# The low-weight pass of a feed-forward matmul: one instruction of 512 tokens, or two of 256

## The reference, cut to what matters

```python
h = modulate(rms_norm(x, g_pre_mlp[l]), sh2, sc2)
y = jnp.square(jax.nn.relu(h @ w_ff1[l])) @ w_ff2[l]
x = x + gt2[:, None, :] * rms_norm(y, g_post_mlp[l])
```

## Time and profile before

| | us |
|---|---|
| median of 3 runs | 2076.68 |
| lowest and highest | 2076.37, 2077.79 |
| span of the profiled execution, first to last instruction | 2076.6 |
| TensorE busy | 2045.0 (98%) |
| VectorE busy | 1599.3 (77%) |
| ScalarE busy | 811.7 (39%) |

### The profile page before, as it was taken

The page is one execution under the profiler, slowest core; times in us unless marked ns, Lnnn a source line. Parts: engine busy times, 40 slices in busy tenths (PEclk is TensorE's granted clock), DMA queues, the critical chain, the costliest instruction groups (busy, mean ns, idle before and its releaser), DMA issues.

```text
span 2076.6 us, 25311 instructions
## 1 busy us (share of the span) xinstructions
PE 2045.0 (98%) x9099; PEld 1670.2 (80%) x9099; DVE 1599.3 (77%) x1843; ACT 811.7 (39%) x1063; POOL 87.7 (4%) x97
## 2 busy tenths in 40 slices
PE   7999999999999999999999999999999999999998
PEld 5787788888778778888888888888888888888886
DVE  7999897776978787687686786776867867867767
ACT  6434622224543364334243343343342433433433
POOL 1001120000220001000000000000000000000000
PEclk9999999999999999999999999999999999999999
DMA  9986568856347843233332332332333323323335
GB/s 368 391 272 194 194 205 290 298 182 201 128 171 266 274 156 112 92 106 103 106 100 91 112 102 91 119 105 97 101 100 112 101 91 111 101 91 113 107 99 197
DMA packets 181600, 324.58 MB, mean 156 GB/s; under 512 B 12601, under 2 KB 49641, under 8 KB 179233
## 3 DMA queue, kind: packets, MB, share of 16 engines
q1 hardware_dynamic: 173600, 302.08, 44.0%
q0 software_dynamic: 3568, 16.95, 2.2%
q10 hardware_dynamic: 4368, 4.73, 0.7%
HBM read 313.20 MB, written 10.52 MB: 156 GB/s over the span
## 4 chain that ended last, share of the span: by engine, by line
PE 90%; DVE 7%; ACT 1%; issue 1%; DMA 0%; DVEq 0%; ACTq 0%
PE pair L939 11%; PE pair L940 11%; PE pair L941 11%; PE pair L964 9%; PE pair L965 9%; PE pair L966 9%; PE bank L568 5%; PE bank L570 5%; PE bank L569 5%; PE bank L580 3%; PE bank L582 3%; PE bank L581 3%; DVE acc L1581 1%; DVE w_lo L1549 1%; DVE stat L1766 1%
## 5 line engine op out<-in xcount | busy, mean ns | idle before, releaser
L2017 DVE TENSOR_TENSOR yg<-yg,pair 128x1024 f32<-128x1024 f32 x240 | 289.6, 1217 | 283.2 <-PE pair L966 283.2
L939 PE MATMUL pair<-h_hi,w_lo 128*128 128x512 f32 x1020 | 397.3, 390 | 0.0
L940 PE MATMUL pair<-h_lo,w_hi 128*128 128x512 f32 x1020 | 396.8, 389 | 0.0
L941 PE MATMUL pair<-h_hi,w_hi 128*128 128x512 f32 x1020 | 396.8, 389 | 0.0
L964 PE MATMUL pair<-w_hi,op_lo 128*128 128x512 f32 x840 | 328.3, 391 | 0.0
L965 PE MATMUL pair<-w_lo,op_hi 128*128 128x512 f32 x840 | 326.9, 389 | 0.0
L966 PE MATMUL pair<-w_hi,op_hi 128*128 128x512 f32 x840 | 326.9, 389 | 0.0
L1072 ACT ACTIVATE w_hi<-raw 128x1024 fp32r<-128x1024 f32 (+1 forms) x114 | 118.3, 1045 | 270.1 <-DMA raw<-in_w_in_dram 155.2
L939 PEld LDWEIGHTS pair<-h_hi,w_lo 128*128 128x128 f32 x1020 | 191.6, 188 | 39.9 <-issue 0.2
L941 PEld LDWEIGHTS pair<-h_hi,w_hi 128*128 128x128 f32 x1020 | 191.5, 188 | 39.9
L940 PEld LDWEIGHTS pair<-h_lo,w_hi 128*128 128x128 f32 x1020 | 191.5, 188 | 39.4
(11 more groups left out here) (295 smaller groups left out, 2803.0 us busy)
## 6 DMA issues: line engine op xcount, KB each, us to landing
raw<-in_w_ada_dram SPq DMA_DIRECT2D x128, 512.0 KB, 4.6
w_raw<-in_w_ff_dram SPq DMA_DIRECT2D x128, 512.0 KB, 3.8
raw<-in_w_ff_dram SPq DMA_DIRECT2D x128, 512.0 KB, 4.4
raw<-in_w_in_dram SPq DMA_DIRECT2D x74, 512.0 KB, 4.7
gst<-in_w_ada_dram SPq DMA_DIRECT2D x64, 512.0 KB, 7.8
raw<-in_w_out_dram SPq DMA_DIRECT2D x32, 512.0 KB, 4.8
x_tok<-in_x_dram SPq DMA_DIRECT2D x4, 1024.0 KB, 8.2
xr<-in_x_dram POOLq DMA_DIRECT2D x4, 1024.0 KB, 7.0
```

The lines of the kernel that those rows point to most:

```text
L939: pe.matmul(b, lo[:, cols], h_hi[:, kt, :], start=(kt == 0), stop=False)
L940: pe.matmul(b, hi[:, cols], h_lo[:, kt, :], start=False, stop=False)
L941: last = pe.matmul(b, hi[:, cols], h_hi[:, kt, :], start=False, stop=(kt == KT - 1))
L2017: dve.tensor_tensor(y, y, pairs[2 + (i + r) % 2][:, :, :], ALU.subtract if i == 6 else ALU.add).then_inc(product_read, 1)
```

## The change

In each block of a piece the high-by-low matmul comes first and opens the accumulation for all 512 tokens. The matmul with the low part of the weights comes second, and is issued as two matmuls of 256 tokens each, with the same stationary operand, into the two halves of the same bank. The high-by-high matmul stays last. Waits and semaphores are the same. `first_piece` and the second product are not touched.

```diff
                     b, cols = pairs[m // 2][:, m % 2, :], slice(m * P, (m + 1) * P)
-                    pe.matmul(b, lo[:, cols], h_hi[:, kt, :], start=(kt == 0), stop=False)
-                    pe.matmul(b, hi[:, cols], h_lo[:, kt, :], start=False, stop=False)
+                    pe.matmul(b, hi[:, cols], h_lo[:, kt, :], start=(kt == 0), stop=False)
+                    for tok in (slice(0, 2 * P), slice(2 * P, 4 * P)):
+                        pe.matmul(b[:, tok], lo[:, cols], h_hi[:, kt, tok], start=False, stop=False)
                     last = pe.matmul(b, hi[:, cols], h_hi[:, kt, :], start=False, stop=(kt == KT - 1))
```

## The result

| | before | after |
|---|---|---|
| median, lowest and highest of 3 runs, us | 2076.68 (2076.37 to 2077.79) | 2090.79 (2090.17 to 2091.58) |
| span of the profiled execution, us | 2076.6 | 2089.0 |

The change makes the kernel 14.1 us slower, ratio 1.0068 with a 95% interval of 1.0048 to 1.0087. Run once more in a later comparison of more runs it gave 2090.74 against 2076.61, ratio 1.0071 (1.0057 to 1.0084). The span grew by 12.4 us only, because the work ahead of the feed-forward block, which is the same in both, took 1.9 us less in the profiled execution of after: its first matmul of the block starts at 748.0, and at 749.9 before. (In every run with both numbers on record, the time lies 1.8 us above its own span, so the profiled execution of before was longer than its median run by some 1.7 us.) From there to the end 14.3 us were added, near the 14.1 of the medians.

A forecast was written before the change was run, and what follows sets the result against it. TensorE's queue was taken to bound the kernel: 1020 splits at 13.3 ns add 13.5 us, 0.7 comes back from the late operand, +12.8 us gives 2089.5 us. The 8-in-10 range was 2076 to 2104 us.

The forecast's parts named there:

- The bound: In the loop TensorE is full, busy 98% of the span, so its queue's cost is nearly one to one the kernel's.
- The price of the added instruction: At line 939's 1020 split matmuls, 13.3 ns per added instruction, +13.5 us in all; chance 0.48.
- the lost beat: Rival: unequal lengths keep the stream disturbed, 5.5 ns more on each of a block's four matmuls; +36 us, 2113 us; chance 0.16.
- the per-column rival: Rival: the 13.2 ns belong to the columns, halves take 113.3 ns, the change adds 0 us, 2076.7 us; chance 0.27.
- What comes back: At line 964 the first product's late low operand is hidden by 0.053 of 0.15 us, 13 to 15 times: -0.7 to -0.8 us.
- The sum: On TensorE's queue 1020 x 13.3 ns, +13.5 us; less 0.7 come back, +12.8 us, 2089.5 us, 0.6% slower.
- Its signs of being wrong: In the trace: halves not 0.12 us apart, 512-column matmuls changing their distance, or a TensorE wait not there before.
- The order of the passes: The opening matmul reads `w_hi` and `h_lo` instead, with all four waits still ahead of it; costs nothing by itself.
- the second load: Each half at line 939 has its own weight load, 109 to 111 ns, which isn't the bound.
- the other engines: ScalarE and VectorE wait for TensorE with 26% and more idle; an iteration 0.85 us longer gives them more.
- the gain: Rival: a half costs no more than its load, a pair 218 to 223 ns; -3.6 to -8.7 us; chance 0.04.
- the slower form: Rival: 256 float32r columns run like float32, a half 213 ns, a pair 426; +204 us, 2280 us; chance 0.03.

## Why the prediction was right, point by point

**The bound.** Right for the loop. TensorE's queue sets the time there: 15.9 us of added work in it give 15.9 us once the one wait is out of the way. The first chunk is not bound by it alone; the prediction counted its 64 splits in full, and they added 0.15 us in place of 0.9.

**The price of the added instruction.** The step that the prediction called the one on which everything hangs, once per instruction or per column, came out as chosen: 13.3 ns per instruction. The rows had not decided it, as the prediction says itself; it was a choice at 0.48 against 0.27, with 0.16 for the lost beat. And the trace of after alone would have misled. Its halves are 115 ns apart, nearer to the 113.3 of the per-column rival than to 119.9, and the sign that the prediction named for it (0.120 between the halves) did not appear. Only the kernel with all passes in halves (120.0) and the one with other lengths (173 and 147) show it.

**The lost beat.** The prediction had it as a rival with 22 ns a block on top of the pair's 13.3. It does happen: the whole matmuls are 233 apart, as the earlier trace rows show behind a late load. What failed is the size. The prediction added 5.5 ns to all four matmuls; the whole ones did get 6.4 each, but in the same state the halves are 4.8 below their settled 120, and 3.3 ns a block are left: 3.4 us in all. This is the term that the forecast lacked.

**What comes back.** Forecast 0.7 us, measured 1.9: the wait cost 2.4 us before and 0.5 after. Two errors. The operand is that of the iteration's second product (it starts at 1214.68, the first at 1209.20), not of the first. VectorE's work up to it hangs on product 12, and two pieces stand between that and the second product, not one. So the operand's cover grew by 8 x 16.65 = 133 ns, and the lateness fell from 0.26 to 0.13. VectorE took as long as before, 9.88 us from the first line to the second:

```profile
1207.07 1.22 DVE L2018 TENSOR_TENSOR yg<-yg,pair 128x1024 f32<-128x1024 f32 x1 [3.67 <-PE pair L967]
...
1216.95 0.69 DVE L1985 TENSOR_TENSOR op_lo<-s_tmp,op_hi 128x512 fp32r<-128x512 f32 x1
```

The other kernels agree: with one block split (2 x 33 ns of cover) the load is 0.20 us late, and with all passes in halves (2 x 180 ns) it is on time. The second error is in the price. A load that was 0.26 us late cost 0.17 us an iteration, one 0.20 late 0.11, and one 0.13 late 0.03. So the cost falls as the lateness does, but it starts from some 0.12 us late and not from 0. That fits an estimate from rows: a load needs some 0.11 us of the matmul's 0.227, so 0.12 us are to spare.

**The sum.** 13.5 - 0.7 = 12.8 was forecast. The account is 15.9 - 1.9 = 14.0 in the loop and 0.15 in the first chunk, and 14.1 was measured. The forecast lacked 3.3 ns a block, gave back 1.2 us too little, and counted some 0.8 us in the first chunk that did not come. These errors partly cancel, so part of the closeness is luck.

**Its signs of being wrong.** It named three: halves not 0.12 apart, another distance of the 512-column matmuls, a wait that was not there. All three are in the trace of after: 0.115, 0.233, and 0.58 us once at line 939. The first two are one thing, the stream out of step, and leave the price per instruction standing; the third was not foreseen and costs little. The time came out near the forecast with the trace not looking as forecast.

**What was costed at nothing.** The order of the passes (2076.43 alone), the second load, which lies beside the matmul, and the other engines: all right. The per-column rival, the gain and the slower form are out: 256 columns run at the columns' full rate, and the load's floor of 112 ns is under 120.

## What to carry to other kernels

Where TensorE's queue is full, count instructions as well as columns: in this float32r stream each costs its columns and 13.3 ns more, down to some 240 columns (112 ns less 13.3 is 98.7 ns of columns), below which its weight load sets 112 ns. Price a new shape in a stream of its own kind, since beside other lengths its cost shows up at its neighbours. And look at how late a wait's data is against what the work in flight covers: a slower engine may pay for part of itself, and putting the late operand first in the queue of the engine that makes it can win the same without it.

## What the runs showed of the hardware that was not expected

- A float32r stream has a settled distance (226.7, 173.3, 146.7 and 120.0 ns for 512, 384, 320 and 256 columns) and states out of step beside it. Behind a group of 2, 8 or 24 halves that followed a settled stream, the whole matmuls came some 233, 236, 228, 232, 231 ns apart and then 227, and the earlier trace rows show much the same behind a load that was late. What is out of step with what is open; nothing here tells.
- Lengths in turn can stay out of step for good: 696.6 ns a block for 512, 256, 256, 512, and 707 for 512, 256, 512, 256, where the settled sum is 693.3 for both.
- A weight load can be late at no price up to a point: beside matmuls 0.227 us apart, 0.13 us late cost 0.03 us, 0.20 late 0.11 and 0.26 late 0.17.
- The 13.3 ns are absent at the lower clock and there at the full one for every length that was tried above the load's floor.
